# Attention on one core: the last tile's values between the two key products of the next head

## The reference, cut to what matters

```python
q = (rmsnorm(c_q, q_norm_g) @ w_uq).reshape(B, S, H, MLA_QK_DIM)
kv = (rmsnorm(c_kv, kv_norm_g) @ w_ukv).reshape(B, S, H, MLA_NOPE_DIM + MLA_V_DIM)
...
s = jnp.einsum('bqhd,bkhd->bhqk', q_blk, k).astype(jnp.float32) * scale
s = jnp.where(mask[None, None], s, neg)
prob = jax.nn.softmax(s, axis=-1).astype(v.dtype)
return jnp.einsum('bhqk,bkhe->bqhe', prob, v)
```

## Time and profile before

| | |
|---|---|
| median of 3 runs | 1255.94 us |
| the profiled execution's own time | 1256.79 us |
| its span, first to last instruction | 1255.0 us |
| TensorE busy | 1235.7 us, 98% of the span |
| VectorE, ScalarE, GpSimd busy | 57%, 39%, 41% |
| mean granted TensorE clock | 0.998 of full speed |
| the four heads of the attention | about 288 to 404 us from the start of the span |
| the three seams | at about 314, 343 and 372 us |

### The profile page before, as it was taken

How to read it: one execution, slowest core, us unless ns; L and a number is a source line. 1 busy time by engine, 2 the same in 40 slices (tenths; PEclk the granted TensorE clock), 3 DMA queues, 4 the chain that set the end, 5 groups by cost and what they waited for, 6 DMA issues and landing times.

```text
span 1255.0 us, 16767 instructions
## 1 busy us (share of the span) xinstructions
PE 1235.7 (98%) x6008; PEld 1040.1 (83%) x6008; DVE 721.2 (57%) x1174; ACT 486.5 (39%) x891; POOL 516.4 (41%) x518
## 2 busy tenths in 40 slices
PE   9999999989999999999999999999999999999997
PEld 8888888878888888888888888888888888888886
DVE  5544444466665427855444455444489999954433
ACT  7622222246665214633333333333354334424422
POOL 3533443351110002555433555434399889810011
PEclk9999999999999999999999999999999999999999
DMA  9511101001012500242422433423554545420002
GB/s 342 160 37 40 45 2 42 1 1 34 17 52 101 151 1 1 76 126 84 126 89 81 125 109 101 126 76 93 184 178 160 183 168 185 151 84 1 1 34 101
DMA packets 101931, 115.09 MB, mean 92 GB/s; under 512 B 4832, under 2 KB 67680, under 8 KB 101856
## 3 DMA queue, kind: packets, MB, share of 16 engines
q1 hardware_dynamic: 101424, 113.57, 27.8%
q10 hardware_dynamic: 432, 0.54, 0.1%
HBM read 90.49 MB, written 23.59 MB: 91 GB/s over the span
## 4 chain that ended last, share of the span: by engine, by line
PE 95%; DVE 2%; ACT 1%; issue 1%; DMA 1%; POOL 0%; SPq 0%; POOLq 0%; DVEq 0%; ACTq 0%
PE PS L1722 11%; PE PS L1723 11%; PE PS L1724 11%; PE PS L206 8%; PE PS L208 8%; PE PS L207 8%; PE PS L2058 5%; PE PS L2057 5%; PE PS L2056 5%; PE PS L1026 3%; PE PS L1042 3%; PE PS L2411 2%; PE PS L2412 2%; PE PS L2413 2%; PE PS L2422 2%; PE PS L861 2%
## 5 line engine op out<-in xcount | busy, mean ns | idle before, releaser
L206 PE MATMUL PS<-WF,HTH 128*128 128x512 f32 (+1 forms) x448 | 176.7, 394 | 2.7 <-DVE WF L184 2.0
L208 PE MATMUL PS<-WF,HTL 128*128 128x512 f32 (+1 forms) x448 | 173.5, 387 | 0.0
L207 PE MATMUL PS<-WF,HTH 128*128 128x512 f32 (+1 forms) x448 | 173.1, 386 | 0.0
L1443 DVE TENSOR_TENSOR X<-X,PS 128x512 f32<-128x512 f32 x172 | 110.3, 679 | 54.6 <-PE PS L208 37.1
L1722 PE MATMUL PS<-HTH,WF 128*128 128x512 f32 x336 | 130.7, 389 | 0.0
L1723 PE MATMUL PS<-HTL,WF 128*128 128x512 f32 x336 | 130.7, 389 | 0.0
L1724 PE MATMUL PS<-HTH,WF 128*128 128x512 f32 x336 | 130.7, 389 | 0.0
L1655 DVE TENSOR_TENSOR WF<-RAW,WF 128x512 fp32r<-128x512 f32 x63 | 70.3, 1117 | 77.5 <-ACT WF L1645 77.5
L206 PEld LDWEIGHTS PS<-WF,HTH 128*128 128x128 f32 x448 | 84.2, 188 | 19.0 <-DVE WF L184 2.5
L1722 PE MATMUL PS<-WF 128*128 128x512 f32 x252 | 98.0, 389 | 0.0
L1723 PE MATMUL PS<-WF 128*128 128x512 f32 x252 | 98.0, 389 | 0.0
(11 more groups left out here) (260 smaller groups left out, 2814.2 us busy)
## 6 DMA issues: line engine op xcount, KB each, us to landing
hid<-TMP SPq DMA_DIRECT2D x74, 256.0 KB, 2.3
TMP<-hid SPq DMA_DIRECT2D x25, 512.0 KB, 4.4
RAW<-in_w_ffn_gate SPq DMA_DIRECT2D x22, 512.0 KB, 4.2
RAW<-in_w_ffn_up SPq DMA_DIRECT2D x22, 512.0 KB, 5.4
RAW<-in_w_ffn_down SPq DMA_DIRECT2D x22, 512.0 KB, 4.1
X<-in_x SPq DMA_DIRECT2D x16, 512.0 KB, 5.7
RAW<-in_w_in SPq DMA_DIRECT2D x32, 256.0 KB, 3.8
TAB<-hid SPq DMA_DIRECT2D x9, 512.0 KB, 4.9
```

Source lines behind the costliest of these rows:

```text
L206: nc.tensor.matmul(dst, HTH[:, k, tok], w_h, start=(k == 0), stop=False)
L207: nc.tensor.matmul(dst, HTH[:, k, tok], w_l, start=False, stop=False)
L208: last = nc.tensor.matmul(dst, HTL[:, k, tok], w_h, start=False, stop=(k == K - 1))
L1443: nc.vector.tensor_tensor(x, x, src, ALU.add).then_inc(done, 1)
```

## The change

In `next_keys` the call for the keys is taken apart: block 0 of the keys first, then the last tile's values, then block 1. It applies at all three seams. The streams of ACT, DVE, POOL and SyncE keep their order, and so do all waits.

```diff
             def next_keys(values, h):
-                head_keys(e, h)
+                head_keys(e, h, [0])
                 values()
+                head_keys(e, h, [1])
             with e.Fori(0, HEADS - 1) as h:
                 pe_head(e, h, lambda b: head_queries(e, h + 1, b), lambda values: next_keys(values, h + 1))
```

## The result

| | median us | runs | span of the profiled execution |
|---|---|---|---|
| before | 1255.95 | 6 (1255.87 to 1256.07) | 1255.0 |
| after | 1261.74 | 6 (1261.64 to 1262.08) | 1260.3 |

The change costs 5.79 us. The ratio after to before is 1.0047, 95% interval 1.0034 to 1.0060. The forecast was 1261.7 us, the range 1259.8 to 1263.2 us. The medians in this document leave out one run at a lower granted clock (1383.37 us at 0.85, of the kernel with the rest of QR and out_hi(7) ahead).

What follows compares the result with a forecast made beforehand. TensorE, busy 98% of the span, was taken as the bound, with a latency chain over ACT and DVE to turn(1) at each seam. Three seams at 1.91 us gave 5.73 us on 1255.94: 1261.7 us, range 1259.8 to 1263.2 us.

Steps and rivals of the forecast that it cites:

- values(7) does not start earlier: At each seam: values(7) waits for ACT's copy, ending at 314.93; removing matmuls gains zero, and TensorE's wait grows to 0.82 us.
- Key block 1 takes 0.70 us behind values(7): TensorE at each seam: three matmuls run behind values(7), 317.04 to 317.73, so scores(0) starts 0.69 us later.
- the lower end: Least cost of a seam, 0.69 us, if ACT and DVE had slack; as the matmuls-only rival 1258.0 us, chance 5%.
- ACT's queue: At each seam, block 1's late copy and the rest of QR stand ahead of out_hi(7), moving it and turn(1) 1.91 us.
- Nothing else moves turn(1): First seam: scores(3) ends at 321.5, divide(0) releases turn(0) at 322.04; DVE's branch stays the later by 0.5 us.
- The third seam counts in full: Third seam, without table load or loop branch: DVE's branch on the edge, so 1.91 us again; lower end 1.4 us.
- No dearer table load: Against the rival of a dearer load behind busy ACT work at two seams: at most 2.6 us, 1264.3 us, chance 3%.
- the prediction's 8.1 us from the page: Estimate with the skill page's 1380 ns drain per table switch: two seams cost some 2.4 us more, 8.1 us in all.
- Nothing gives it back: Behind the seams no time is regained: TensorE is solid from 408 us on and releases the other engines.
- TensorE does not take block 1 past the waiting values(7): Against the rival that block 1's matmuls fill the 0.82 us gap ahead of values(7): 1255.6 or 1255.9 us, chance 4%.

## Why the prediction was right, step by step

- *values(7) does not start earlier.* Right: ACT's copy ends at 314.71 and values(7) starts at 314.81. TensorE's wait ahead of it is 0.81 us, 0.82 were forecast.
- *Key block 1 takes 0.70 us behind values(7).* Right (0.72 us in this seam). In the sum it stands as a delay of ACT, and there it counts in full. But I also called 0.69 us a seam the lower end, and alone these matmuls cost 0.28 to 0.67 us. TensorE had slack of 0.4 us ahead of turn(1) at the loop's seams; turn(1) stands behind DVE there, so that bound was wrong.
- *ACT's queue.* Right as mechanism. The size was 1.91 us a seam and measured 1.83. One term was mis-sized: the copy of block 1 starts 0.02 us behind TensorE's last matmul (317.55, 317.57), where I took the 0.13 us of out_hi(7). The three matmuls took 0.72 us instead of 0.69, and from the copy of block 1 to out_hi(7) it is 1.22 us from start to start, as worked out (1.21 to 1.22).
- *Nothing else moves turn(1).* Right: TensorE ends scores(3) at 321.24, divide(0) releases turn(0) at 321.75, a margin of 0.5 us as forecast.
- *The third seam counts in full.* Right: 1.83 us.
- *No dearer table load.* Right. The load stands behind busy work now and takes 1.28 us. The drain of 1380 ns in the Trainium skill, "ScalarE: Activation LUTs", section "What ACT_TABLE_LOAD costs", is not in this trace: exp(0) starts 320.52 - 320.35 = 0.17 us behind the load, and DVE's bias is what it waits for. That section gives the drain for a switch to a different set. The loads at the two seams are none: with the loop written out, they fall away and nothing takes their place. So the prediction's 8.1 us from the page took it for a case that it does not speak of. The load ahead of head 0 stays when the loop is written out, and exp(0) is 0.01 us behind it.
- *Nothing gives it back.* Right: behind the third seam both executions take 877.1 us.
- *TensorE does not take block 1 past the waiting values(7).* Right: block 1 starts at 316.59, when values(7) runs out, after 0.81 us in which TensorE stood with those matmuls behind.

The forecast of 1261.7 us against 1261.74 us is closer than its parts, and that closeness is luck. The sum was 5.73 us where the seams gave 5.50, 0.08 us too much at each. The medians lie 0.29 us above the seams: that is the scatter of executions shown above (0.84 - 0.34 - 0.21 us), and it made up for the sum's excess. The mechanism, ACT's queue with DVE behind it, is not luck: holding ACT alone gives 1.13 us a seam with TensorE's order untouched.

## What to carry to other kernels

When a producer's instruction is moved behind another, look at the consumer's queue first: the price is not the moved work but all that stands in order behind the consumer's wait. Here three matmuls of 0.70 us alone cost 1.3 us over three seams, and held ACT and DVE make it 5.8 us. A long instruction group that waits anyway (values(7) behind a copy) is the place to have all other engines' inputs ready before it, not after it. If an order can't be kept, take whatever does not need the late input ahead of the wait; that alone gave back 2.1 us.

## What the runs showed that I had not expected

- A hardware loop over three heads costs about 1.2 us here against the same code written out (1254.62 against 1255.83 us); 0.4 us at each of two seams is seen in the traces, and 0.4 us is not located. The largest part at a seam is DVE's idle time of 0.35 us between two passes, after a last instruction that has waited. Behind a last instruction of 0.69 us it is not seen. The written-out kernel also has no table load at these seams, and shorter steps from TensorE to ACT and from ACT to DVE.
- The releaser that the profile names for biggest(0), TensorE's scores, was not what held it: scores(0) came 0.69 us later and biggest(0) 0.18 us.
- In the changed order a ready group of matmuls stood for 0.81 us behind a waiting one, at three seams of three; with values(7) ahead of both key blocks, six of them stood for 1.66 us at the first seam. Order was kept.
